# First modulation columns summed on the vector engine, S5 input weights built on GpSimd, in a two-block transformer on one Trainium2 core

## The reference

```python
c_act = silu(c)
mod = c_act @ mod_w[layer] + mod_b[layer]            # 1024 x 6144
sh_m, sc_m, gt_m, sh_f, sc_f, gt_f = split(mod, 6)
h = x * (1 + sc_m) + sh_m
u, q, k, v, g_out, a_low = split(h @ w_in[layer])    # 1024 x 2064
y = concat([s5(u, lam, log_dt, b, c, d, w_glu), gla(q, k, v, g_out, a_low)]) @ w_out[layer]
x = layer_norm(alpha * x + (1 + gt_m) * y)
...                                                   # feed-forward, then layer 2, then the second block
# s5: lam_bar = exp(lam * dt); b_bar = ((lam_bar - 1) / lam) * b   (complex, 32 groups x 64 states x 16 channels)
```

## Time and profile before

| | |
|---|---|
| median of 3 runs | 2794.58 us (2790.4 to 2800.55) |
| span of the profiled execution | 2788.6 us, 32539 instructions |
| time of the profiled execution outside its span | not shown; the median of the runs lies 6.0 us above the span |
| PE busy | 2530.0 us (91%), DVE 2080.7 us (75%), ACT 1461.2 us (52%), POOL 18.0 us (1%) |
| HBM read | 594.87 MB, 214 GB/s over the span |
| end of the stage "start" | 133.8 us |

### The profile page before, as it was taken

How to read it: one execution, slowest core, us unless ns; L and a number is a source line. 1 busy time by engine, 2 the same in 40 slices (tenths; PEclk the granted TensorE clock), 3 DMA queues, 4 the chain that set the end, 5 groups by cost and what they waited for, 6 DMA issues and landing times.

```text
span 2788.6 us, 32539 instructions
## 1 busy us (share of the span) xinstructions
PE 2530.0 (91%) x12413; PEld 2026.9 (73%) x12413; DVE 2080.7 (75%) x2254; ACT 1461.2 (52%) x1535; POOL 18.0 (1%) x29
## 2 busy tenths in 40 slices
PE   5989689998686999999999999998888999988998
PEld 2736567777455788888888888876777887767787
DVE  5588787665766899989898988997865554776554
ACT  1221433442233777777777787775544544454543
POOL 0001000000000000000000000000000000000000
PEclk9997899998697999999999999999989999999999
DMA  7451246654132899999999999995403553503452
GB/s 239 154 184 66 91 171 250 243 211 127 46 121 76 307 356 360 347 361 356 345 361 372 371 358 355 359 348 191 139 31 106 166 187 110 196 1 106 136 183 89
DMA packets 274343, 598.12 MB, mean 214 GB/s; under 512 B 28722, under 2 KB 37248, under 8 KB 273026
## 3 DMA queue, kind: packets, MB, share of 16 engines
q1 hardware_dynamic: 252144, 580.30, 58.7%
q10 hardware_dynamic: 22034, 15.67, 2.0%
HBM read 594.87 MB, written 1.06 MB: 214 GB/s over the span
## 4 chain that ended last, share of the span: by engine, by line
PE 64%; DVE 26%; ACT 4%; issue 2%; ACTq 2%; DMA 2%; DVEq 0%; POOLq 0%
PE PS L215 62%; DVE WL L171 6%; PE PS L237 2%; DVE MW L171 2%; DVE WF L171 2%; DVE AR L171 2%; ACTq L150 2%; ACT WH L207 2%; DVE MOD L171 1%; DVE HF L171 1%; DVE H L171 1%; DVE SMALL L182 1%; DVE AR L179 1%; DVE HTR L171 1%; ACT AR L207 1%
## 5 line engine op out<-in xcount | busy, mean ns | idle before, releaser
L171 DVE TENSOR_TENSOR WL<-RG,WH 128x1024 fp32r<-128x1024 f32 (+1 forms) x558 | 919.2, 1647 | 371.2 <-ACT WH L207 339.0
L207 ACT ACTIVATE WH<-RG 128x1024 fp32r<-128x1024 f32 (+1 forms) x558 | 781.7, 1401 | 615.4 <-PE PS L215 552.7
L215 PE MATMUL PS<-WH,HTR 128*128 128x512 f32 (+2 forms) x2920 | 847.6, 388 | 40.9 <-DVE HTR L171 13.7
L215 PEld LDWEIGHTS PS<-WH,HTR 128*128 128x128 f32 x2920 | 551.3, 191 | 154.5 <-DVE HTR L171 15.3
L215 PE MATMUL PS<-WL,HTR 128*128 128x512 f32 (+2 forms) x1460 | 506.8, 385 | 1.4 <-DVE WL L171 1.4
L215 PE MATMUL PS<-WH,ATR 128*128 128x512 f32 x1624 | 457.9, 394 | 17.5 <-DVE WL L171 9.4
L215 PEld LDWEIGHTS PS<-WH,ATR 128*128 128x128 f32 x1624 | 305.9, 189 | 82.6 <-DVE WL L171 16.0
L215 PE MATMUL PS<-MW,HTR 128*128 128x512 f32 x1332 | 330.0, 395 | 1.0 <-DVE MW L171 0.5
L215 PEld LDWEIGHTS PS<-WL,HTR 128*128 128x128 f32 x1460 | 279.0, 191 | 55.5 <-DVE WL L171 2.7
L215 PEld LDWEIGHTS PS<-MW,HTR 128*128 128x128 f32 x1332 | 244.5, 188 | 55.3 <-DVE MW L171 6.5
L171 DVE TENSOR_TENSOR MW<-RG,MW 128x2048 fp32r<-128x2048 f32 x112 | 256.8, 2292 | 12.5 <-ACT MW L207 0.6
(11 more groups left out here) (230 smaller groups left out, 1993.9 us busy)
## 6 DMA issues: line engine op xcount, KB each, us to landing
RG<-in_moe_w_gate SPq DMA_DIRECT2D x112, 1024.0 KB, 6.9
RG<-in_moe_w_up SPq DMA_DIRECT2D x112, 1024.0 KB, 6.7
RG<-in_moe_w_down SPq DMA_DIRECT2D x112, 1024.0 KB, 6.8
RG<-in_w_ff SPq DMA_DIRECT2D x64, 1024.0 KB, 5.0
RG<-in_mod_w SPq DMA_DIRECT2D x48, 1024.0 KB, 5.2
RG<-in_w_in SPq DMA_DIRECT2D x34, 1024.0 KB, 6.1
RG<-in_w_out SPq DMA_DIRECT2D x16, 1024.0 KB, 5.1
RG<-in_ffn_w_gate SPq DMA_DIRECT2D x14, 1024.0 KB, 5.2
```

Of the source, the lines that this page charges most:

```text
L171: return self.did(lambda: self.e.tensor_tensor(o, a, b, op))
L207: return self.did(lambda: self.e.activation(o, a, f, bias=bias, scale=scale))
L215: return self.did(lambda: self.e.matmul(o, l, r, start=start, stop=stop))
```

## The change

1. The plan of loads begins with eight raw loads ("first", k) of 128x2048, one for each 128 rows of mod_w, in the place of the eight blocks of four by 512 columns. DVE sums them into HROW (`v_first`), and the PE forms the 16 columns with `COL` (a column of ones). `pe_mod(pe, 0)`, `a_mod(a, 0)` and `v_mod(v, 0)` go. CZ and CBC are written at the end of `v_first`.
2. The turns of mod_b and the LN rows, and the 16 turns of X, come first in `pe_first`, ahead of the columns. The strings of "start" are new.
3. `g_s5_in` takes the place of `v_s5_in` for both layers; the PE waits on `sw_g` for its results. GpSimd runs it for layer 0 before its first fence.
4. For layer 0 SP issues the six S5 loads, ahead of all weight loads; for layer 1 ACT still does. The jobs of layer 0 come as `JOBS0`: C, then B and K for each k.
5. The row loads of ACT (`a_w_in_rows`, 2.3 MB) are issued ahead of the copies of weights.

```diff
-    ("mixers0", "g"): "gggggggggggggg",
+    ("mixers0", "g"): "bbbbgggggggbggggggg",
...
-    ("start", "a"): "prrrrrrrpprrprrprrppppppppppppppppppppppp",
-    ("start", "pe"): "rpppppprpprrprrrrpprrrprppprrrrppppppppppppppppppp",
-    ("start", "v"): "rprrrrrrrrrrrrrrpppprrppprrpppprpprppppppppppppppppppp",
+    ("start", "a"): "prrrrpppppppppppppppppppprpprrppprrpppppprrrrrr",
+    ("start", "pe"): "pppppppppppppppprrppprrpprrrppprrrppprrrrrrrr",
+    ("start", "v"): "ppprrpprpppprrppppppppppprpprpprpprpprppprrpppprppprpppprrrrr",
...
-        plan_mod(0, 0, 4)
+        for k in range(8):
+            W.plan(("first", k), w["mod_w"][0, k * 128:(k + 1) * 128, 0:2048], 1, 2048, raw=W.raw_first)
         for l in range(L):
...
+        JOBS0 = [("C", z) for z in range(2)] + [x for k in range(4) for x in (("B", k, 0), ("B", k, 1), ("K", k))]
         JOBS = [("B", k, z) for k in range(4) for z in range(2)] + [("C", z) for z in range(2)] + [("K", k) for k in range(4)]
...
-        def a_s5_in(a, l):
+        def s5_in(eng, l):
             if l:
-                a.wait_ge(s5_pe, 0, "u1")
+                eng.wait_ge(s5_pe, 0, "u1")
             for dst, src in ((XBS[l][0][:, 0], w["s5_b_re"][l].rearrange("(j g) p h -> (g p) j h", g=2)),
                              (XBS[l][0][:, 1], w["s5_b_im"][l].rearrange("(j g) p h -> (g p) j h", g=2)),
...
-                a.dma(dst, src).then_inc(s5_bc_in)
+                eng.dma(dst, src).then_inc(s5_bc_in)
...
                     elif x[0] == "B":
-                        pe.wait_ge(sw_v, l, f"bd{x[1]}")
+                        pe.wait_ge(sw_g, l, f"bd{x[1]}")
                         m = pe.tr(o, BDS[l][:, x[1], x[2], 4 * q:4 * q + 4].rearrange("p i g h -> p (i g h)"), IDN)
                     else:
+                        pe.wait_ge(sw_g, l, f"bd{x[1]}")
                         pe.wait_ge(sw_v, l, "jobC1")
...
-        def v_s5_in(v, l):
-
-            yield
-            v.wait_ge(s5_bc_in, 6 * (l + 1))
+        def g_s5_in(g, l):
+
+            yield
+            g.wait_ge(sw_v, 0, "PC")
+            g.wait_ge(s5_bc_in, 6 * (l + 1))
             if l:
                 for j in range(4):
-                    v.wait_ge(s5_pe, 0, f"v{j}")
+                    g.wait_ge(s5_pe, 0, f"v{j}")
             src = XBS[l][0]
             for k in range(4):
+                if k:
+                    yield
                 dst = XBS[l][(k + 1) % 2]
                 a_, b_ = (P_CR, P_CI) if k == 0 else AB[0]
+                g.tt(dst[:, 0], src[:, 0], col(l, a_, 16), MUL)
+                g.tt(XT, src[:, 1], col(l, b_, 16), MUL)
+                g.tt(dst[:, 0], dst[:, 0], XT, SUB)
+                g.tt(dst[:, 1], src[:, 1], col(l, a_, 16), MUL)
+                g.tt(XT, src[:, 0], col(l, b_, 16), MUL)
+                g.tt(dst[:, 1], dst[:, 1], XT, ADD)
                 hm = KC[:, K_HM:K_HM + 2].unsqueeze(1).unsqueeze(3).broadcast_to([128, 16, 2, 16])
                 for z in range(2):
-                    y = v.tt(BDS[l][:, k, z], dst[:, z].unsqueeze(2).broadcast_to([128, 16, 2, 16]), hm, MUL)
-                y.then_inc(sw_v, f"bd{k}")
+                    y = g.tt(BDS[l][:, k, z], dst[:, z].unsqueeze(2).broadcast_to([128, 16, 2, 16]), hm, MUL)
+                y.then_inc(sw_g, f"bd{k}")
                 src = dst
-                yield
...
         def v_s5_cx(v, l):
+            v.wait_ge(s5_bc_in, 6 * (l + 1))
...
-        def v_s5_next(v):
-            yield from v_s5_out(v, 0)
-            yield from v_s5_in(v, 1)
-
         def pe_mixers(pe, l):
             weave(pe, f"mixers{l}", s=pe_s5(pe, l), g=pe_gla(pe, l), m=pe_mods(pe, l))
 
         def v_mixers(v, l):
             weave(v, f"mixers{l}", s=v_s5(v, l), g=v_gla(v, l), m=v_mods(v, l),
-                  b=iter(()) if l else v_s5_next(v))
+                  b=iter(()) if l else v_s5_out(v, 0))
 
         def a_mixers(a, l):
             weave(a, f"mixers{l}", s=a_s5(a, l), g=a_gla(a, l), m=once(lambda: a_mod(a, 6 if l else 3)),
-                  b=once(lambda: (a_second_in(a), a_ln_rows(a, 1, "mix", 1))) if l else once(lambda: a_s5_in(a, 1)))
+                  b=once(lambda: (a_second_in(a), a_ln_rows(a, 1, "mix", 1))) if l else once(lambda: s5_in(a, 1)))
 
         def g_mixers(g, l):
-            weave(g, f"mixers{l}", g=g_gla(g, l))
+            weave(g, f"mixers{l}", g=g_gla(g, l), b=iter(()) if l else g_s5_in(g, 1))
...
         def pe_first(pe):
-            yield from pe_mod(pe, 0)
             yield
             pe.wait_ge(first_in, 6)
             pe.tr(PS[:, 7, 0:96], CB[0:96, 128:256], KC[0:96, K_ID:K_ID + 96])
             pe.tr(PS[:, 7, 96:160], CB[0:64, 256:384], KC[0:64, K_ID:K_ID + 64]).then_inc(pro_pe)
             yield
             pe.wait_ge(pro_v, 1)
-            pe.wait_ge(mod_v, 1)
-            yield from pe_w_in(pe, 0)
+            yield from pe_h_mod(pe, 0)
+            yield
+            pe.wait_ge(*W.of["first", 7][0].raw)
+            for j in range(16):
+                x = pe.mm(PS[:, 3, j:j + 1], HROW[:, j * 128:(j + 1) * 128], COL[:, 1:2], True, True)
+            x.then_inc(mod_pe, "columns0")
+            yield from pe_project(pe, ("w_in", 0), BLOCKS1, FIRST[0], lambda k: pe.wait_ge(hm_v, 0, f"l{k // 2}"))
 
         def pe_w_in(pe, l):
             yield from pe_h_mod(pe, 2 * l, lambda t: pe.wait_ge(ln_v, 1, f"n{t}") if l else None)
             yield from pe_project(pe, ("w_in", l), BLOCKS1, FIRST[l], lambda k: pe.wait_ge(hm_v, 2 * l, f"l{k // 2}"))
 
         def v_first(v):
+            for k in range(8):
+                yield
+                ld = W.of["first", k][0]
+                v.wait_ge(W.landed[ld.slot], ld.use)
+                if k == 0:
+                    v.ts(HROW, ld.dst[:, 0, :], sm(24, 1), None, MUL).then_inc(W.raw_first)
+                else:
+                    v.stt(HROW, ld.dst[:, 0, :], sm(24 + k, 1), HROW, MUL, ADD).then_inc(W.raw_first)
             yield
             v.wait_ge(pro_pe, 1)
             v.cp(MB, PS[:, 7, 0:96])
             v.cp(LNC, PS[:, 7, 96:160]).then_inc(pro_v)
             yield
-            v_mod(v, 0)
-            for _ in range(4):
-                yield
-                W.los(v, 1)
+            v.wait_ge(mod_pe, 0, "columns0")
+            v.tt(MC[:, 0:16], PS[:, 3, 0:16], MB[:, 0:16], ADD).then_inc(mod_v)
+            v.ts(MC[:, 8:16], MC[:, 8:16], 1.0, None, ADD)
             yield from v_w_in(v, 0)
+            yield
+            v.ms(CZ, 0.0)
+            v.cp(CZ[:, :, 3], sm(24, 8))
+            for k in range(8):
+                x = v.ts(CBC[:, k, :], KC[:, K_ONE:K_ONE + 128], sm(24 + k, 1), None, MUL)
+            x.then_inc(silu_v, "c")
 
         def v_w_in(v, l):
-            yield from v_h_mod(v, 2 * l, l, 1, (lambda: W.los(v, 1)) if l else (lambda: None))
+            yield from v_h_mod(v, 2 * l, l, 1, lambda: W.los(v, 1))
             rest = v_ln_rest(v, 1, X) if l else None
             yield from v_project(v, ("w_in", l), BLOCKS1, PR1, AHEAD1, (lambda j: run(rest, 1)) if l else (lambda j: None))
 
         def a_first(a):
             yield
-            a_mod(a, 0)
+            a_w_in_rows(a, 0)
             for _ in range(4):
                 yield
                 W.his(a, 1)
             yield from a_w_in(a, 0)
 
-        def a_w_in(a, l):
+        def a_w_in_rows(a, l):
             for dst, src in ((ROWS[:, O_HG:O_HG + 512], rowb(w["gla_head_gain"][l, :])),
                              (SMALL[:, 40:42], w["gla_b_alpha"][l, :].rearrange("(c p) -> p c", p=128)),
                              (ST[0:16, 128:384], w["gla_w_alpha_up"][l, :, :])):
@@ -3404,25 +3424,26 @@
             if l == 0:
                 a_ln_rows(a, 0, "mix", None)
                 a_gate_bias(a)
+
+        def a_w_in(a, l):
+            if l:
+                a_w_in_rows(a, 1)
             yield from a_h_mod(a, 2 * l)
             yield from a_project(a, ("w_in", l), BLOCKS1, PR1, AHEAD1)
 
         def pe_s5_first(pe):
             yield from pe_s5_rows(pe)
-            yield from pe_s5_jobs(pe, 0, S5_BANKS[0], JOBS)
+            yield from pe_s5_jobs(pe, 0, S5_BANKS[0], JOBS0)
 
         def v_s5_first(v):
             yield from v_s5_rows(v)
-            yield from v_s5_in(v, 0)
             yield
             v_s5_cx(v, 0)
-            yield from v_s5_jobs(v, 0, S5_BANKS[0], JOBS)
+            yield from v_s5_jobs(v, 0, S5_BANKS[0], JOBS0)
 
         def a_s5_first(a):
             yield from a_s5_rows(a)
-            yield
-            a_s5_in(a, 0)
-            yield from a_s5_jobs(a, 0, S5_BANKS[0], JOBS)
+            yield from a_s5_jobs(a, 0, S5_BANKS[0], JOBS0)
...
-            v.ms(CZ, 0.0)
-            v.cp(CZ[:, :, 3], sm(24, 8)).then_inc(silu_v, "c")
             v.wait_ge(consts_in, 1)
-            for k in range(8):
-                v.ts(CBC[:, k, :], KC[:, K_ONE:K_ONE + 128], sm(24 + k, 1), None, MUL)
...
             g.ms(sm(300, 1), 0.0)
+            run(g_s5_in(g, 0))
...
```

(16 more changed lines are left out.)

6 lines of the change are left out of this document (removed).

## The result

The changed kernel takes **2814.28 us** (median of 5 runs, 2810.55 to 2820.08), the kernel before, beside it, 2800.55 us (5 runs). The ratio is 1.0064, with a 95% interval of 1.0044 to 1.0084: slower by 0.64%. Run again in another group it was 2817.42 against 2795.73 us, 1.0086 (1.0064 to 1.0108). The forecast was 2797 us, no change that can be told, with a range up to 2813; the result lies above it.

The account below looks back on a forecast made before the run. The PE was taken as the main bound (64% of the chain, DVE 26%). "start" ending 3.6 us later, less 0.8 us in "mixers0", gave +2.8 us: median 2797 us, 8-in-10 range 2783 to 2813.

Parts of the forecast that it names:

- The issue on SP and the sums: Early in "start": SP issues six S5 loads in 7.3 us; the last of eight HROW sums ends at 43.4 us.
- SP held like ACT: Rival, stage "start": the six loads take 23.6 us to issue on SP, not 7.3, giving 2813 us; chance 0.15.
- From the sums to the projection: Stage "start": turns of X begin at 48.2, columns take 5, the projection starts at 62.1 us, 19 us earlier.
- The projection and the jobs: Stage "start": projection with woven-in S5 jobs takes 61.3 us, PE waiting 1 us; 16-column part ends at 123.4 us.
- The end of the stage: K2, B3, K3 and the last fetch close "start": it ends at 137.4 us, 3.6 us later than before.
- GpSimd for layer 0: Stage "start": GpSimd's four S5 steps take 31 us, have 10 us of cover, and cost nothing.
- "mixers0": Stage "mixers0": DVE loses 16.9 us of operations, but the PE waits little for DVE, so 0.8 us is saved.
- the rule weighed: Skill rule that DVE two-SBUF-input instructions contend with GpSimd; set aside because GpSimd's product took 0.72 us beside 17 DVE operations.
- DVE bounds mixers0 after all: Rival, "mixers0": chain runs through DVE operations that leave; 12.6 us won, not 0.8, 2785 us; chance 0.17 with early sums.
- GpSimd late: Rival, stage "start": each of GpSimd's 32 operations waits out a DVE operation, giving 2826 us, 2807 at half; chance 0.08.

Follow-up runs that it names:

- Run 1: Changed kernel with only the orders of DVE and ScalarE in stage "start" moved, fetches ahead of weight parts: 2798.44 us, 1.0013.
- run 6: Kernel before with only layer 1's S5 input weights built on GpSimd in "mixers0": 2799.36 us against 2795.73, 1.0014.
- run 11: Kernel before with only layer 0's six S5 loads issued by SP ahead of all weight loads: 2789.66 us, 0.9978.
- run 2: Changed kernel with layer 1's S5 input weights back on DVE in "mixers0": 2814.63 us, 1.0062.
- run 7: Changed kernel with the orders of DVE and ScalarE in "start" moved and layer 1's S5 weights back on DVE: 2797.62 us, 1.0008.
- run 10: Changed kernel with DVE's and ScalarE's orders in "start" moved and six of eight operations per GpSimd step in "mixers0" executed twice: 2798.29 us, 1.0017.

## Why the prediction was wrong

- **The issue on SP and the sums**: right (8.3 us for 7.3, last sum end 43.7 for 43.4). The rival "SP held like ACT" did not come about.
- **From the sums to the projection**: the turns as put (48.72 for 48.2, 3.68 us for 3.9), the columns 6.83 us for 5, near the bound of 7.7 at half speed. The 5.0 us behind them were 7.09: I let the projection start at the first low part of X, but it waits for the second, which stands behind a WL and two more scalings on DVE. The start is 66.11, 4.0 us late, of which the columns are inside the bounds I gave and the second low part is in none.
- **The projection and the jobs**: this is the step that failed. I put 61.3 us, with one wait of 1 us, and it took 73.0 (66.11 to 139.1). The waits before B01 and K1 are 8.85 us, the two K jobs at half speed 3.5 us more, and the wait of 1 us for the rows did not come: 61.3 + 8.85 + 3.5 - 1 = 72.7. I had counted DVE's 27 operations against the PE's parts and costed B and K jobs by their matmuls alone. I never followed a fetch: which bank a job waits for, behind which part the fetch of that bank stands, and what that part waits for on the third engine. The two orders of DVE and ScalarE show it without any trace. Run 1 shows it by 15.65 us.
- **The end of the stage**: 13.3 us (139.1 to 152.43) for 14.0, as forecast, with the wait before K2 of 2.21 us.
- **GpSimd for layer 0**: its cost on the path was nothing, as put, and it was done at 122.5 us after 31.7 us of work (31 forecast). But its neighbour paid: four of the five WL beside it took 1.47 to 1.68 us, one took 1.23 like those without it.
- **"mixers0"**: -0.8 us forecast, about +5 in the traces (226.0 against 221.2). Two steps failed. The first is the reading of the earlier trace rows: the 0.8 us there is the longest wait of the PE for one product (WF from L179), not for DVE. In the kernel before, the PE waits for DVE in the same window for 8.06 and 3.03 us:

```profile
176.93 1.09 PE L237 MATMUL PS<-KC,WF 128*128 128x128 f32 x4 [8.06 <-DVE WF L171]
...
192.99 0.40 PE L215 MATMUL PS<-AR,HF 128*63 128x128 f32 x2 [3.03 <-DVE HF L171]
```

Both waits end before DVE's first S5 operation for layer 1 at 197.54 us, so taking these operations away could not shorten them. But GpSimd's first three steps (186.96 to 214.76 us in the changed kernel) run beside the very products that the PE waits for, and there the waits are 9.58 and 5.93 us. On the kernel before with that one part changed (run 6) the PE's waits for WF and HF in the stretch sum to 20.3 us, where they were 14.8; the PE was also busy for 4.5 us more there, at a granted clock of 0.82 where it was 0.85. The second step that failed is the rule weighed. I took from the earlier trace rows that GpSimd and DVE do not disturb each other. The group of 17 hid it. The same rows of the kernel before, cut in windows, are these (line, engine, shapes, count, busy, mean ns), up to 214 us and then to 216:

```profile
L171 DVE TENSOR_TENSOR WF<-WF 128x128 f32<-128x128 f32 x4 | 1.2, 292 | 0.1
...
L171 DVE TENSOR_TENSOR WF<-WF 128x128 f32<-128x128 f32 x3 | 1.8, 607 | 0.1
L171 DVE TENSOR_TENSOR WF<-WF 128x256 f32<-128x256 f32 x2 | 1.4, 691 | 0.2
```

The same DVE product takes 292 ns before GpSimd's first product at 213.3 us begins and 607 ns on the mean once GpSimd works (the mean of three, some of them while GpSimd paused). I had read GpSimd's 0.72 us, which was the side that did not pay, and compared DVE's 128x256 with nothing. The Trainium skill, "SBUF — State Buffer", section "Who interferes with whom", says that a DVE instruction with two SBUF inputs contends with a GpSimd instruction that reads SBUF, and that one with at most one SBUF input doesn't, outside the 2-port perf modes. The trace agrees with both halves: HF<-HF takes 1.22 us without GpSimd and up to 1.65 us beside it in the lines above, HF<-AR,PS 2.48 us in either case. GpSimd paid too: single operations of it in "mixers0" took up to 2.59 us where 0.62 to 0.73 is usual. How two such instructions share the time when they meet, no run here isolates.
- **The rivals**: "DVE bounds mixers0 after all" got 0.17 and is refuted by run 6: nothing was won. DVE was waited for in the stage, but ahead of the operations that left, and the freed time became idle time. In the changed kernel DVE waits for the PE behind the HF chain for 6.50 and 3.78 us, where the kernel before has S5 operations. "GpSimd late" names the right mechanism (contention) in the wrong place and with the wrong victim: GpSimd was not late for anyone.

What remains open: why the medians of runs 2, 7 and 10 do not follow the 4 to 5 us of their traces. The spread behind the stretch can hide them; that it does was not tested. So the contention is shown where it happens, and its price in the whole time is not.

## What to carry to other kernels

Where several engines work off orders of their own, follow every fetch that frees a buffer: behind what it stands on its engine, and what that waits for elsewhere. A fetch that is released by way of two other engines' orders costs the PE the length of that way each time (4.20 and 4.65 us here), and the matmuls behind the pause a slower clock as well. When the trace shows one wait, look at all waits for that engine in the window before a term is put at nothing. Before work is moved to GpSimd, cut a group of DVE instructions that ran beside GpSimd into windows with and without it; a mean over the group, or GpSimd's own duration, does not show who pays. And take a change of several parts apart: here one part, the loads' queue, was a gain by itself (run 11) and was buried under the others.
